# Two-block transformer kernel: operands of the last norm moved into PSUM, and the work between the output projection and the second block's gated network written in another order

## The reference

```
merged = sigmoid(gate_a) * y_a + sigmoid(gate_r) * y_r
x = x + merged @ w_o
h2 = rmsnorm(x, g_ffn)                                   # x * rsqrt(mean(x*x) + eps) * g_ffn
x = x + (silu(h2 @ w_ff_gate) * (h2 @ w_ff_up)) @ w_ff_down    # inner width 2816
return rmsnorm(x, g_final)
```

## Time and profile before

| what | value |
|---|---|
| median of 3 runs (lowest, highest) | 1565.17 us (1564.59, 1566.33) |
| the profiled execution's own time | 1565.51 us |
| its span, first to last instruction | 1563.7 us |
| mean granted TensorE clock | 0.993 |
| PE busy | 1531.8 us, 98% of the span |
| DVE, ACT, POOL busy | 841.2, 406.4, 1000.2 us |
| DMA | 172.56 MB, mean 110 GB/s |

### The profile page before, as it was taken

The page is one execution under the profiler, slowest core; times in us unless marked ns, Lnnn a source line. Parts: engine busy times, 40 slices in busy tenths (PEclk is TensorE's granted clock), DMA queues, the critical chain, the costliest instruction groups (busy, mean ns, idle before and its releaser), DMA issues.

```text
span 1563.7 us, 22486 instructions
## 1 busy us (share of the span) xinstructions
PE 1531.8 (98%) x7888; PEld 1314.6 (84%) x7888; DVE 841.2 (54%) x1100; ACT 406.4 (26%) x682; POOL 1000.2 (64%) x794
## 2 busy tenths in 40 slices
PE   7999999999999999999999999999997999999997
PEld 6998888888887888888888888888886999999887
DVE  7876455560427565244154565556577877875013
ACT  6542111110110001112032122212334555553001
POOL 4736666666666666766556576475565777776664
PEclk9999999999999999999999999999998999999999
DMA  9962333333332333332323232232232233333331
GB/s 373 404 237 81 94 102 99 94 95 94 101 111 84 97 102 97 106 95 81 106 68 95 78 94 82 79 94 80 67 95 67 86 103 107 107 107 94 95 100 62
DMA packets 218123, 172.56 MB, mean 110 GB/s; under 512 B 5216, under 2 KB 191968, under 8 KB 218080
## 3 DMA queue, kind: packets, MB, share of 16 engines
q1 hardware_dynamic: 218080, 171.98, 35.2%
HBM read 169.86 MB, written 2.10 MB: 110 GB/s over the span
## 4 chain that ended last, share of the span: by engine, by line
PE 91%; DVE 4%; DMA 2%; ACT 1%; issue 1%; POOL 1%; SPq 0%; POOLq 0%; DVEq 0%; ACTq 0%
PE ps L790 30%; PE ps L793 30%; PE ps L794 30%; DMA gates<-in_w_mod_t 1%; DMA res<-in_x 1%; DVE gates L1681 0%; DVE act_lo L1772 0%; DVE tmp L2100 0%; POOL w_lo L670 0%; POOL tmp L677 0%; DVE wide_lo L1694 0%; DVE tmp L2102 0%; DVE act_lo L2120 0%; PE ps L874 0%; PE ps L1182 0%
## 5 line engine op out<-in xcount | busy, mean ns | idle before, releaser
L701 POOL TENSOR_TENSOR w_lo<-raw,w_hi 128x1024 fp32r<-128x1024 f32 x204 | 507.7, 2489 | 17.0
L790 PE MATMUL ps<-act_hi,w_hi 128*128 128x512 f32 (+1 forms) x1128 | 419.1, 372 | 4.2 <-POOL w_lo L734 3.9
L793 PE MATMUL ps<-act_hi,w_lo 128*128 128x512 f32 (+1 forms) x1128 | 416.3, 369 | 0.0
L794 PE MATMUL ps<-act_lo,w_hi 128*128 128x512 f32 (+1 forms) x1128 | 416.3, 369 | 0.0
L698 POOL TENSOR_TENSOR w_hi<-raw,zero 128x1 fp32r<-128x1 f32 x204 | 47.6, 234 | 420.4 <-PE ps L790 420.1
L790 PEld LDWEIGHTS ps<-act_hi,w_hi 128*128 128x128 f32 x1128 | 213.8, 190 | 41.9 <-POOL w_lo L734 4.4
L793 PEld LDWEIGHTS ps<-act_hi,w_lo 128*128 128x128 f32 x1128 | 213.9, 190 | 35.9 <-issue 1.2
L794 PEld LDWEIGHTS ps<-act_lo,w_hi 128*128 128x128 f32 x1128 | 213.8, 190 | 35.5
L790 PE MATMUL ps<-wide_hi,w_hi 128*128 128x512 f32 (+2 forms) x624 | 240.0, 385 | 1.8 <-POOL w_lo L701 1.4
L793 PE MATMUL ps<-wide_hi,w_lo 128*128 128x512 f32 (+2 forms) x624 | 239.4, 384 | 0.0
L794 PE MATMUL ps<-wide_lo,w_hi 128*128 128x512 f32 (+2 forms) x624 | 239.4, 384 | 0.0
(11 more groups left out here) (241 smaller groups left out, 2500.2 us busy)
## 6 DMA issues: line engine op xcount, KB each, us to landing
raw<-in_w_in SPq DMA_DIRECT2D x88, 512.0 KB, 4.1
gates<-in_w_mod_t SPq DMA_DIRECT2D x20, 1024.0 KB, 11.4
raw<-in_w_ffn_up SPq DMA_DIRECT2D x40, 512.0 KB, 3.9
raw<-in_w_ffn_down SPq DMA_DIRECT2D x22, 512.0 KB, 3.8
raw<-in_w_ff_gate SPq DMA_DIRECT2D x22, 512.0 KB, 3.8
raw<-in_w_ff_up SPq DMA_DIRECT2D x22, 512.0 KB, 3.9
raw<-in_w_ff_down SPq DMA_DIRECT2D x22, 512.0 KB, 3.8
raw<-in_w_r_out SPq DMA_DIRECT2D x16, 512.0 KB, 3.4
```

The costliest lines, as they stand in the source:

```text
L701: nc.gpsimd.tensor_tensor(w_lo[:, two, :], raw[:, slot, :], f32(w_hi[:, two, :]), SUB).then_inc(split_done, 1)
L790: ins = mm(o, w, a, start=start, stop=False)
L793: mm(o, wl, a, start=False, stop=False)
L794: return mm(o, w, al, start=False, stop=stop)
```

## The change

- The whole scaled tile `gained_psum(m)` is written by ACT over the bank that the projection has left, instead of half a tile into `tmp`. DVE reads it there for the token sums and for the lo part of the activation; PE's tile m+4, which reuses the bank, waits for that lo part (`act_ready[2]`) and no longer for the addition to `res`.
- `t_sums` moves from `tmp` to PSUM banks 2 and 3. The squares of tiles 1 to 6 are written to PSUM bank 1; those of tiles 0 and 7 stay in `tmp`. ACT squares ahead of the sums' hi part. F1's first product, which overwrites bank 1, waits for the sixth addition of squares. `token_sums` waits for the lo part of the sums before.
- Pair 0: the copy and F5's hi part are made at m = 4, F7, F2, F1 at m = 5, F6 at m = 6. F5 comes straight from POOL's sum in `tmp`, and its lo part is made by POOL. The sums of DVE use bank 0 in place. `add3` comes at m = 7. The matmul of the norm follows F7 instead of F6; `half_copy` comes ahead of F3 and F4.
- DVE's reciprocal comes behind the lo part of F6 of pair 1. For pairs 1, 2 and 3 `join` u and vw come ahead of the scaling of the value of the pair before; these three periods are written out ahead of the loop.

```diff
-LO_POOL = {"first": (F7, F2, F1, F4), "later": (F1, F7, F2, F4)}
-LO_DVE = {"first": ("add6", F5, F6, "add3", F3), "later": ("add6", F6, F5, "add3", F3)}
+LO_POOL = {"first": (F7, F2, F5, F1, F4), "later": (F1, F7, F2, F4)}
+LO_DVE = {"first": ("add6", F6, "add3", F3), "later": ("add6", F6, F5, "add3", F3)}
...
-        t_parts = tmp[:, 2:4, :].rearrange("p s t -> p (s t)")
-        half_gained, t_sums = t_parts[:, 0:HALF], t_parts[:, HALF:4 * HALF].rearrange("p (i t) -> p i t", i=3)
+        t_sums = ps[:, 2:4, :].rearrange("p s t -> p (s t)")[:, HALF:4 * HALF].rearrange("p (i t) -> p i t", i=3)
...
-            return ps[:, 2 if is_first(p) else 6, :]
+            return ps[:, 0 if is_first(p) else 6, :]
+
+        def gained_psum(m):
+            return ps[:, 4 + m % 4, :]
+
+        square_psum = ps[:, 1, :]
...
                     if first and form in (F6, F2, F5):
-                        pe.wait_ge(wo_free, {F6: 8, F2: 5, F5: 6}[form])
+                        pe.wait_ge(act_ready[2], {F6: 8, F2: 5, F5: 6}[form])
+                    elif first and form == F1:
+                        pe.wait_ge(squares_added[2], KT - 2)
...
-                        if first and form == F6:
+                        if first and form == F7:
                             norm(2, [3])
...
                 if m >= 4:
-                    pe.wait_ge(wo_free, m - 3)
+                    pe.wait_ge(act_ready[2], m - 3)
...
             for m in range(KT):
                 act.wait_ge(wo_free, m + 1)
-                if m:
-                    act.wait_ge(t_summed, LOADED + m)
-                do(half_gained, res[:, m, halves[0 if m < QUAD else 1]], ACT.Identity, scale=col("g_ffn_2", m)).then_inc(half_scaled, 1)
+                do(gained_psum(m), res[:, m, :], ACT.Identity, scale=col("g_ffn_2", m)).then_inc(gained, 1)
                 tokens = halves[0] if m < QUAD else slice(0, T)
                 hi_of(act_hi[:, m, tokens], res[:, m, tokens], norm_hi_made[2], scale=col("g_ffn_2", m))
+                if m < KT - 1:
+                    res_square(m)
                 act.wait_ge(t_summed, LOADED + m + 1)
...
-                square(2, m)
+                if m == QUAD:
+                    sum_copy(pair0)
+                    form_hi_of(F5, pair0)
                 if m == KT - 3:
-                    sum_copy(pair0)
-                    for form in (F5, F7, F2, F1, F6):
+                    for form in (F7, F2, F1):
                         form_hi_of(form, pair0)
+                if m == KT - 2:
+                    form_hi_of(F6, pair0)
+            res_square(KT - 1)
+            half_copy(pair0)
             form_hi_of(F3, pair0)
             form_hi_of(F4, pair0)
-            half_copy(pair0)
...
-                dve.wait_ge(half_scaled, LOADED + m + 1)
+                dve.wait_ge(gained, LOADED + m + 1)
+                if m:
+                    dve.wait_ge(t_ready, m)
...
-                stt(out=act_lo[:, m, tokens], in0=res[:, m, tokens], scalar=col("g_ffn_2", m), in1=f32(act_hi[:, m, tokens]),
-                    op0=MUL, op1=SUB).then_inc(act_ready[2], 1)
+                tt(act_lo[:, m, tokens], gained_psum(m)[:, tokens], f32(act_hi[:, m, tokens]), SUB).then_inc(act_ready[2], 1)
                 token_lo(m)
-                add_squares(2, m)
+                if m == KT - 1:
+                    add3((0, 0))
+                if m:
+                    dve.wait_ge(res_squared[2], m + 1)
+                    tt(tmp[:, 0, :], square_psum if m < KT - 1 else tmp[:, 1, :], tmp[:, 0, :], ADD).then_inc(squares_added[2], 1)
+                    dve.wait_ge(squares_added[2], m)
                 if m == KT - 3:
                     add6((0, 0))
-                    form_lo_dve_of(F5, (0, 0))
                 if m == KT - 2:
                     form_lo_dve_of(F6, (0, 0))
-                    add3((0, 0))
...
+            join("u", pair0)
             add6(later(pair0))
-            join("u", pair0)
             join("vw", pair0)
+            form_lo_dve_of(F6, later(pair0))
             rstd(2, tmp[:, 4, :])
-            form_lo_dve_of(F6, later(pair0))
             form_lo_dve_of(F5, later(pair0))
...
-            with dve.Fori(0, FT // 2 - 1) as i:
-                for p in ((i, 1), (i + 1, 0)):
-                    dve_period(p)
+            for j in range(1, 4):
+                dve_period(pair_of(j), behind=True)
+            with dve.Fori(2, FT // 2 - 1) as i:
+                for o in range(2):
+                    dve_period((i, o))
+            dve_period(pair_of(FT - 2))
```

More of the change, by code:

```diff
@@ L140, in counted @@
 def counted(order, p, what):
-    n = number(p)
-    kind = order["first"] if is_first(p) else order["later"]
-    return LOADED + n * len(kind) + kind.index(what) + 1
+    first, later_ = order["first"], order["later"]
+    if is_first(p):
+        return LOADED + first.index(what) + 1
+    return LOADED + len(first) + (number(p) - 1) * len(later_) + later_.index(what) + 1
 def joined_at(p, what):
@@ L714, in add5 @@
                 if not is_first(p):
-                    pool.wait_ge(form_hi_made, counted(HI, earlier(p), "copy"))
+                    last = earlier(p)
+                    pool.wait_ge(form_hi_made, counted(HI, last, F5 if is_first(last) else "copy"))
+                    if is_first(last):
+                        pool.wait_ge(form_lo_pool, counted(LO_POOL, last, F5))
                 nc.gpsimd.tensor_tensor(sum5, v[:, A1], v[:, A2], ADD).then_inc(form_summed, 1)
@@ L745, in _ @@
             form_lo_of(F2, pair0)
+            form_lo_of(F5, pair0)
             form_lo_of(F1, pair0)
@@ L972, in form_ready @@
                 def form_ready(form, p):
-                    if form in LO_POOL["later"]:
+                    if form in LO_POOL["first" if is_first(p) else "later"]:
                         pe.wait_ge(form_lo_pool, counted(LO_POOL, p, form))
@@ L1512, in form_hi_of @@
                     act.wait_ge(form_summed, LOADED + number(p) * 2 + 2)
+                elif form == F5 and is_first(p):
+                    act.wait_ge(form_summed, LOADED + 1)
                 elif form == F5:
@@ L1544, in seven_wide, with res_square @@
                 hi_of(wide_hi[:, ds(number(p), 1), :].rearrange("p o t -> p (o t)"), value_psum(p[1]), prod_hi_made[1])
+            def res_square(m):
+                if m >= 2:
+                    act.wait_ge(squares_added[2], m - 1)
+                do(tmp[:, 0, :] if m == 0 else square_psum if m < KT - 1 else tmp[:, 1, :], res[:, m, :], ACT.Square
+                   ).then_inc(res_squared[2], 1)
             pair0 = (0, 0)
@@ L2098, in token_sums @@
                 k = m - QUAD
-                link(stt(out=t_sums[:, 0, :], in0=res[:, k, halves[1]], scalar=col("g_ffn_2", k), in1=half_gained, op0=MUL, op1=SUB))
+                link(stt(out=t_sums[:, 0, :], in0=res[:, k, halves[1]], scalar=col("g_ffn_2", k), in1=gained_psum(m)[:, halves[1]],
+                         op0=MUL, op1=SUB))
                 link(stt(out=t_sums[:, 1, :], in0=res[:, k, halves[0]], scalar=col("g_ffn_2", k), in1=t_sums[:, 0, :],
@@ L2190, in _, with dve_period @@
             form_lo_dve_of(F3, later(pair0))
-            def dve_period(p, make=True):
+            def dve_period(p, make=True, behind=False):
                 join("c2", earlier(p))
@@ L2196, in dve_period @@
                     add6(later(p))
+                if behind:
+                    join("u", p)
+                    join("vw", p)
                 seven_value(earlier(p))
                 seven_product(earlier(p))
-                join("u", p)
+                if not behind:
+                    join("u", p)
                 if make:
@@ L2202, in dve_period @@
                 seven_wide_lo(earlier(p))
-                join("vw", p)
+                if not behind:
+                    join("vw", p)
                 if make:
```

12 lines of the change are left out of this document (6 added, 6 removed).

## The result

The changed kernel takes 1554.99 us (median of 4 runs, 1553.80 to 1555.38), the kernel before 1565.75 beside it (4 runs). The ratio is 0.9930 with a 95% interval of 0.9913 to 0.9947: about 11 us faster. Forecast were 1548.3 and a range of 1545.9 to 1552.8. The profiled execution took 1555.38 us with a span of 1553.6.

The account below looks back on a forecast made before the run. TensorE, busy 98% of the span, was taken as the bound. Of 19.25 us lost between projection tile 6 and F6 of pair 2, 2.4 would stay, so 1565.17 - 16.9 = 1548.3 us, range 1545.9 to 1552.8.

Parts of the forecast that it names:

- the panel split's wait: PE's 1.4 us wait for POOL's last panel split goes; bounds 0 to 0.3 us left.
- F1: First wait, pair 0: of 3.9 us, 1.1 stay, for the sixth addition of squares; bounds 0.5 and 2.
- F2's last step: Second wait, 4.0 us, for `act_lo` of m = 7: 0.2 us stay; bounds 0 and 1.
- F4 of pair 1: Wait of 2.9 us for `join` vw: 0.5 us stay; bounds 0 and 2.9.
- F6 of pair 2: May wait for its hi part, made by ACT behind a later product: 0.3 us, bounds 0 and 0.5.
- the clock: With no wait above 1.1 us left in the transition, all 5.95 us lost to half clock go.
- the price of a PSUM operand: DVE instructions reading one input from PSUM instead of SBUF cost 0 extra.
- The second rival: PSUM operands cost what the VectorE page says: 18 instructions from m = 5 some 60 ns longer; 1549.5 us, chance 0.04.
- there nothing can be won, and whatever is won earlier shifts everything behind it: From 1240 to 1420 PE is busy 180.0 of 180.0 us at full clock, so no gain or loss was counted there.
- The first: Rival: F4 of pair 1 waits over 2.5 us behind the reciprocal's chain, clock falls; +2.5 and 3.3/2, 1552.5 us, chance 0.12.
- The fourth: Rival, slower: steady loop loses its step, F4 waits 19 times; at 1.2 us a pair 1571 us; chance 0.02.
- PE waits beyond 1240: Sign that the forecast is wrong: PE waiting in the stretch after 1240, where it was busy throughout before.

Follow-up runs that it names:

- e6: Changed kernel with the low part of act again made by VectorE's scalar_tensor_tensor from res in SBUF instead of PSUM; 1557.73 us, ratio 0.9953.
- e8: As e6 against the changed kernel, with the squares also put in SBUF (`tmp`) again; 1558.57 us, ratio 0.9957.
- e1: Changed kernel with VectorE's steps of pairs 4 to 7 also written out, the loop starting at pair 8; 1553.93 us, ratio 0.9930.
- e13: Changed kernel with VectorE's reciprocal again ahead of the low part of F6 of pair 1; 1554.70 us, ratio 0.9937.
- e10: Changed kernel with ScalarE's F6 high part ahead of the previous product's rounding, and silu behind the next pair's F4 high part and sum copy; 1552.13 us.
- e11: e10 with u and vw ahead of the previous pair's value and product on VectorE in all pairs; 1552.17 us, ratio 0.9917.
- e3: Changed kernel with u and vw ahead of the previous pair's value and product on VectorE in all pairs from 1 to 20; 1550.86 us, ratio 0.9914.

## Why the prediction was wrong

**What held.** The cause (VectorE's two SBUF inputs beside GpSimd) is shown by e6 and e8. In the transition each term came within its bounds:

- the panel split's wait: 0 forecast, none measured;
- F1: 1.1 forecast, pitch 1.32 where 0.23 is due, 1.1; the chain from tile 6's addition to the end of its squares took 5.41 (1185.52 to 1190.93) against 5.4;
- F2's last step: 0.2 and 0.15 (no wait is listed, but its first matmul starts 0.27 behind the one before where 0.12 is due, 1194.93 to 1195.20); ScalarE's wider scaled tile takes 0.69 us in PSUM, 0.11 more than the 0.58 of the earlier trace rows, for which 0.1 was added;
- F4 of pair 1: 0.5 and 0.76, from the reciprocal's start to vw's end 10.38 (1201.30 to 1211.68) against 10.4;
- F6 of pair 2: 0.3 and 0.28;
- the clock: 1.00 throughout;
- the price of a PSUM operand: 0 forecast, and 682 ns measured where the same line had 747 at its least with both in SBUF. The second rival, the 1.2 us worked out from the table of the Trainium skill ("VectorE: DVE Perf Modes", The TRN2 errata), did not come: the chain in the item on F1 took what was counted without it.

Together 16.45 of 16.85. One sum is slightly off: the last panel split, from 1177.01 with 2.92 and 3.75, ends at 1183.68 and not 1183.65; nothing hangs on it.

**What failed** is the sentence "there nothing can be won, and whatever is won earlier shifts everything behind it", and with it "pairs 3 to 21 are untouched". PE busy at full clock in a stretch says that nothing is lost in it *as VectorE arrives there now*. Before, VectorE paid its lag at F4 of pair 1 (2.9 us and half clock) and entered the next pairs with its order intact. The change puts off that payment. I checked whether TensorE waits for vw in pair 1, and gave no thought to how late VectorE still is when it gets there. The pace of the recovery was in the trace of before. VectorE's sixth addition of pair 2 starts there at 1221.05, and then:

```profile
1225.54 0.68 DVE L2146 TENSOR_TENSOR decay<-tmp,ps 128x512 f32<-128x512 f32 x1
...
1230.66 0.70 DVE L2078 TENSOR_TENSOR ps<-ps,raw 128x512 f32<-128x512 f32 x1 [0.59 <-ACT ps L1529]
```

The ordinary step is 9.61 us against 10.08, so it recovers 0.47 in a pair, and vw stands 4.49 behind the sixth addition, 3.3 later than with u and vw first. Three pairs could recover 1.4 at the best, so a wait of up to 1.9 us at pair 4 was to be expected even if the new step had been no longer than the old. It was longer, and recovered nothing: in place of the 0 that the prediction has for all that lies behind F6 of pair 2, 4.75 us were lost.

**The rivals.** The first, a wait of over 2.5 us with half clock behind it, came in kind and size (2.66, and 1.7 for the clock where 1.65 was reckoned), three pairs behind the place named. It was priced as a longer chain behind the reciprocal, while the real mechanism is the switch back. The fourth named VectorE's entry into the loop from "written-out periods with another order", and was looked at only as a loss in every pair. The sign that came, PE waits beyond 1240, was named among those that would make the prediction wrong.

## What to carry to other kernels

A wait that goes away by reordering is not paid, only put off, if the late engine's own period is no shorter than the bottleneck's: work out both periods and see in which pair the lag falls due, above all where the order switches back. A full engine behind a wait says nothing of how full it stays when the wait is removed. And when an engine runs late because an operation of little use to it stands ahead of what others wait for, as the rounding ahead of F6's high part, putting that one behind gives it the slack to catch up (4.4 us here, for one moved line).

## What was not expected of the hardware

- The same wait of 2.66 to 2.68 us at F4 of pair 4 was followed by half clock in the changed kernel and e1 (granted clock 0.76 from 1243 to 1250) and in e8 a little later (0.83 from 1250 to 1260), and by none in e6 and e13 (1.00), whose programs are alike there. The half clock behind one and the same wait costs 1.7 us or does not come. Differences of this size between single profiles are no evidence until the clock row has been looked at. e6 and e13:

```profile
1243.00:1250.00 7.00, 4.34 (x36) 4.14 (x35) 6.00 (x11) 3.89 (x8) 5.56 (x5) 1.00 0.34 94
```

```profile
1243.00:1250.00 7.00, 4.33 (x36) 4.13 (x35) 5.91 (x10) 4.47 (x9) 5.31 (x6) 1.00 0.41 118
```

- Moving one silu added two table loads of 1.28 us each to every second pair (e10, e11).
- VectorE's step with u and vw first is 10.2 us written out and 10.08 inside the loop (e3). In the loop of e3 VectorE has no listed wait for TensorE, only 0.6 us for ScalarE's copy and 1.25 for F6's high part in each step, and TensorE none for VectorE; yet both take 10.08. Whose pace it is no run tells apart.
